# TensorE turns the identity matrix in front of its waits, and the norms turn early tiles whole

## The reference

```python
# first block
hn = rms_norm(h, mix_norm_pre);  proj = hn @ w_in          # 8 projections, 3272 columns
ret_out = retention(rope(rq), rope(rk), rv, rg)            # 8 heads, chunks of 128
att_out = dsa_attention(rope(aq), rope(ak), av, iq, ik, iw)  # top-k 128 keys per query, then softmax
h = h + rms_norm(concat(ret_out, att_out) @ w_out, mix_norm_post)
up = causal_dwconv(rms_norm(h, ffn_norm_pre) @ w_up)       # 2 x 2816 columns
h = h + rms_norm((silu(g) * u) @ w_down, ffn_norm_post)
# second block: every norm is followed by (1 + scale) and shift from c; every result gets a gate
x = x + gate * hgrn2_mixer(modulate(x));   x = x + gate * swiglu(modulate(x))
shared = nsa_shared_kv(modulate_kv(x))                     # compressed, selected and window keys
x = x + gate * nsa_mixer(modulate(x), shared);  x = x + gate * swiglu(modulate(x))
```

## Time and profile before

| | |
|---|---|
| median of 3 runs | 2125.06 us |
| profiled execution | 2125.37 us |
| its span | 2123.5 us, 30783 instructions |
| busy: PE, PE weight load, DVE, ACT, GpSimd | 2041.9, 1672.3, 1251.0, 798.1, 81.2 us |
| mean granted PE clock | 0.985 of 2.4 GHz |

### The profile page before, as it was taken

How to read it: one execution, slowest core, us unless ns; L and a number is a source line. 1 busy time by engine, 2 the same in 40 slices (tenths; PEclk the granted TensorE clock), 3 DMA queues, 4 the chain that set the end, 5 groups by cost and what they waited for, 6 DMA issues and landing times.

```text
span 2123.5 us, 30783 instructions
## 1 busy us (share of the span) xinstructions
PE 2041.9 (96%) x12072; PEld 1672.3 (79%) x12072; DVE 1251.0 (59%) x2209; ACT 798.1 (38%) x1455; POOL 81.2 (4%) x79
## 2 busy tenths in 40 slices
PE   7999899999999999999999999999899999999998
PEld 6688678888887877787888888779767678888887
DVE  4577757777745449755545545676777756322334
ACT  3323643333424552244222232433457743222222
POOL 1012000000000002000000000001001100000000
PEclk9999899999999999999999999999899999999999
DMA  6221024655442231202664644322300025233221
GB/s 209 96 83 41 18 92 160 199 191 166 159 148 90 90 100 62 81 21 90 199 197 159 203 153 166 122 84 79 122 1 2 2 79 166 92 100 99 99 90 50
DMA packets 146699, 231.48 MB, mean 109 GB/s; under 512 B 7325, under 2 KB 83709, under 8 KB 146557
## 3 DMA queue, kind: packets, MB, share of 16 engines
q1 hardware_dynamic: 144300, 224.05, 32.0%
q0 software_dynamic: 864, 3.15, 0.4%
q10 hardware_dynamic: 1392, 2.33, 0.3%
HBM read 227.41 MB, written 2.10 MB: 108 GB/s over the span
## 4 chain that ended last, share of the span: by engine, by line
PE 83%; DVE 9%; ACT 3%; issue 3%; POOL 0%; DMA 0%; ACTq 0%; DVEq 0%; POOLq 0%
PE ps L2304 11%; PE ps L2306 11%; PE ps L2305 11%; PE ps L2546 4%; PE ps L2331 4%; PE ps L2333 4%; PE ps L2332 4%; PE ps L2262 4%; PE ps L2264 4%; PE ps L2263 4%; PE ps L2544 3%; PE ps L2618 3%; PE ps L2387 2%; PE ps L2352 2%; PE ps L2364 2%
## 5 line engine op out<-in xcount | busy, mean ns | idle before, releaser
L1588 DVE TENSOR_TENSOR w_lo<-ring,w_hi 128x1024 fp32r<-128x1024 f32 (+4 forms) x362 | 376.9, 1043 | 701.8 <-ACT w_hi L990 701.2
L990 ACT ACTIVATE w_hi<-ring 128x1024 fp32r<-128x1024 f32 (+4 forms) x362 | 329.5, 912 | 970.5 <-PE ps L2306 471.9
L2304 PE MATMUL ps<-x_hi,w_hi 128*128 128x512 f32 x1056 | 416.5, 394 | 0.0
L2306 PE MATMUL ps<-x_hi,w_lo 128*128 128x512 f32 x1056 | 411.3, 389 | 0.0
L2305 PE MATMUL ps<-x_lo,w_hi 128*128 128x512 f32 x1056 | 411.2, 389 | 0.0
L2305 PEld LDWEIGHTS ps<-x_lo,w_hi 128*128 128x128 f32 x1056 | 198.6, 188 | 42.4 <-issue 1.9
L2304 PEld LDWEIGHTS ps<-x_hi,w_hi 128*128 128x128 f32 x1056 | 198.6, 188 | 42.3 <-issue 1.9
L2306 PEld LDWEIGHTS ps<-x_hi,w_lo 128*128 128x128 f32 x1056 | 198.3, 188 | 42.0
L2331 PE MATMUL ps<-w_hi,x_hi 128*128 128x512 f32 x480 | 187.5, 391 | 3.7 <-DVE x_hi L1664 3.7
L2333 PE MATMUL ps<-w_hi,x_hi 128*128 128x512 f32 x480 | 186.8, 389 | 0.0
L2332 PE MATMUL ps<-w_lo,x_hi 128*128 128x512 f32 x480 | 186.8, 389 | 0.0
(11 more groups left out here) (344 smaller groups left out, 2980.3 us busy)
## 6 DMA issues: line engine op xcount, KB each, us to landing
ring<-in_ada_w SPq DMA_DIRECT2D x48, 1024.0 KB, 5.0
ring<-in_ffn_w_in SPq DMA_DIRECT2D x88, 512.0 KB, 4.6
ring<-in_w_up SPq DMA_DIRECT2D x44, 512.0 KB, 4.6
ring<-in_ffn_w_out SPq DMA_DIRECT2D x20, 1024.0 KB, 4.7
ring<-in_hgrn_w_in SPq DMA_DIRECT2D x16, 1024.0 KB, 5.2
ring<-in_w_in SPq DMA_DIRECT2D x12, 1024.0 KB, 5.0
ring<-in_w_down SPq DMA_DIRECT2D x10, 1024.0 KB, 4.9
ring<-in_kv_ada_w SPq DMA_DIRECT2D x8, 1024.0 KB, 5.0
```

Of the source, the lines that this page charges most:

```text
L990: a.activation(to[:, n % depth, 0:src.shape[-1]], src, ACT.Copy).then_inc(s["hi_done"], 1)
L1588: v.tensor_tensor(to[:, n % depth, 0:width], src, hi[:, n % depth, 0:width].bitcast(F32), ALU.subtract).then_inc(s["lo_done"], 1)
L2304: mm(bs[j], wh[:, k, c], x_hi[:, 2 * q + k], start=first, stop=False)
L2306: ins = mm(bs[j], wl[:, k, c], x_hi[:, 2 * q + k], start=False, stop=last)
```

## The change

- `keep_busy(b, n, t)` turns the identity n times into a bank that PE holds anyway and that the next real result overwrites. It is put: in `norm`, ahead of the wait for a tile, by a table `BUSY`; ahead of the first piece of P1 (14), of the HGRN and NSA projections (12 each) and of each FFN (12); in the sparse attention ahead of each wait for an exponential (3) and of each pair of value products (3); in `q_turn` ahead of both turns (5 each); in the compressed groups ahead of the turn (6) and of the value product (4). Where a bank was opened behind a wait, it is opened ahead of it.
- `norm` turns channels 4 to 7 of tiles 0 and 1 once tile 1 is there, and all channels of tiles 2 and 3 as they come.
- The first FFN piece of unit 0 waits for one channel block, and goes through all four columns with it before the second block.
- Norm 0: `vec` moves to bank 7 and is turned behind tile 1; DVE copies it behind its second tile; ACT makes the second early `w_hi` behind channel block 1. The banks of P1's first unit are 0 to 3 in order.
- SP waits for x tile 1 before it issues the first weights. GpSimd issues its two rows after the rotation adds of P1.
- Norm 4: DVE no longer waits for the last turned block before it splits the first, and `XN[4]` lies in another part of the arena.

```diff
+            def keep_busy(b, n, t=0):
+                for _ in range(n):
+                    tr(b[:, t * P:(t + 1) * P], ident, ident)
...
+            BUSY = {0: (15, 0, 0, 0), 1: (0, 36, 0, 0), 2: (0, 36, 0, 0), 3: (0, 13, 7, 0), 4: (0, 0, 0, 13), 5: (0, 13, 7, 0)}
             def norm(i):
                 banks = [open_bank(("xT", i, kt)) for kt in range(4)]
-                for t in range(NT):
-                    pe.wait_ge(s["xn_ready"], NT * i + t + 1)
-                    for kt in range(4):
+                def tiles(t, kts):
+                    for kt in kts:
                         ins = tr(banks[kt][:, t * P:(t + 1) * P], XN[i][:, t, kt * P:(kt + 1) * P], ident)
                         if t == NT - 1:
                             ins.then_inc(full(("xT", i, kt)), 1)
-                for kt in range(4, KT):
-                    turn(lambda t: XN[i][:, t, kt * P:(kt + 1) * P], ("xT", i, kt))
+                for t in range(2):
+                    keep_busy(banks[0], BUSY[i][t], t)
+                    pe.wait_ge(s["xn_ready"], NT * i + t + 1)
+                    tiles(t, range(4))
+                if i == 0:
+                    vec_turn()
+                banks += [open_bank(("xT", i, kt)) for kt in range(4, KT)]
+                for t in range(2):
+                    tiles(t, range(4, KT))
+                for t in range(2, NT):
+                    keep_busy(banks[0], BUSY[i][t], t)
+                    pe.wait_ge(s["xn_ready"], NT * i + t + 1)
+                    tiles(t, range(KT))
...                                                        # ffn
+                        if (u, q) == (0, 0):
+                            keep_busy(open_bank(keys[0]), 12)
                         pe.wait_ge(s["lo_done"], n + 1)
-                        if u == 0:
+                        if u == 0 and q:
                             pe.wait_ge(s["x_split"], (KT + FT) * i + 2 * q + 2)
...
+                        if (u, q) == (0, 0):
+                            steps = [(j, k) for k in range(2) for j in range(4)]
+                        for j, k in steps:
+                            if (u, q) == (0, 0) and j == 0:
+                                pe.wait_ge(s["x_split"], (KT + FT) * i + k + 1)
...                                                        # attention
+                            if name == "dsa":
+                                keep_busy(b[:, at:], 3)
+                            pe.wait_ge(s["p_ready"], base + i + 1)
...
+                        if name == "dsa":
+                            keep_busy(b, 3, slot)
                         for q in range(2):
                             evacuated(pe, t_key(name, i + q, pair[q]["n"]))
...                                                        # P1, HGRN, NSA projections
+                    keep_busy(open_bank((name, 0)), 14)
+            keep_busy(open_bank((*H_UNITS[0], 0)), 12)
+            keep_busy(open_bank((*N_UNITS[0], 0)), 12)
...                                                        # q_turn, compressed groups
+                    b = open_bank(("nT", i, n))
+                    keep_busy(b, 5)
...
+                    b = open_bank(("cT", i - 1))
+                    keep_busy(b, 6)
...
+                    b = open_bank(("cO", i - 2))
+                    keep_busy(b, 4)
...                                                        # SP, ACT, DVE
+                if n == 0:
+                    sp.wait_ge(s["x_in1"], 16)
...
-                    early_highs(0, slice(0, 2))
+                    early_highs(0, slice(0, 1))
...
-                filled(dve, ("xT", i, KT - 1))
```

More of the change, by code:

```diff
@@ L270, in build @@
         INDEX_UNIT = P1_ORDER.index("rk")
-        plan_bank("vec")
+        plan_bank("vec", 7)
         def plan_norm(i):
@@ L397, in build @@
         plan_norm(0)
+        turn[0] = 1
         P1_PIECES = [(k, q) for k in range(len(P1_ORDER)) for q in range(4)]
@@ L406, in build @@
             for t in range(NT):
-                plan_bank((name, t), 4 * (k % 2) + ((t + 1) % NT if k == 0 else t))
+                plan_bank((name, t), 4 * (k % 2) + t)
             if k == 0:
@@ L957, in norm_out @@
                                      bias=0.0 if shift is None else shift[:, kt:kt + 1]).then_inc(free(("xT", i, kt)), 1)
+                        if kt == 1:
+                            early_highs(i, slice(1, 2) if i == 0 else slice(0, 0))
                     return
@@ L1372, in norm @@
                         x_normed(0, t)
+                        if t == 1:
+                            p = filled(dve, "vec")
+                            v.tensor_copy(vec[:, 0:CONV], p[:, 0:CONV]).then_inc(free("vec"), 1)
                 if i in MIXER_NORM:
@@ L2214, in _, with vec_turn @@
             tr = nc.tensor.transpose
+            def keep_busy(b, n, t=0):
+                for _ in range(n):
+                    tr(b[:, t * P:(t + 1) * P], ident, ident)
             pe.wait_ge(s["ident_in"], 16)
-            pe.wait_ge(s["vec_rows_in"], 16 * len(VEC_ROWS))
-            b = open_bank("vec")
-            tr(b[:, 0:64], vec_rows, ident[0:64, 0:64]).then_inc(full("vec"), 1)
+            def vec_turn():
+                pe.wait_ge(s["vec_rows_in"], 16 * len(VEC_ROWS))
+                b = open_bank("vec")
+                tr(b[:, 0:64], vec_rows, ident[0:64, 0:64]).then_inc(full("vec"), 1)
             def other_rows():
@@ L2293, in ffn @@
                         n = split_at[("up", i, u, q)]
+                        if (u, q) == (0, 0):
+                            keep_busy(open_bank(keys[0]), 12)
                         pe.wait_ge(s["lo_done"], n + 1)
-                        if u == 0:
+                        if u == 0 and q:
                             pe.wait_ge(s["x_split"], (KT + FT) * i + 2 * q + 2)
                         wh, wl = [w[:, n % 2].rearrange("p (k n) -> p k n", k=2) for w in (w_hi, w_lo)]
-                        for j in range(4):
-                            if q == 0:
+                        steps = [(j, k) for j in range(4) for k in range(2)]
+                        if (u, q) == (0, 0):
[3 more added lines that the diff above has]
+                                pe.wait_ge(s["x_split"], (KT + FT) * i + k + 1)
+                            if (q, k) == (0, 0):
                                 bs[j] = open_bank(keys[j])
                             c = slice(j * P, (j + 1) * P)
[L2302 to L2307, removed]
+                            first, last = (q, k) == (0, 0), (q, k) == (3, 1)
+                            mm(bs[j], wh[:, k, c], x_hi[:, 2 * q + k], start=first, stop=False)
+                            mm(bs[j], wh[:, k, c], x_lo[:, 2 * q + k], start=False, stop=False)
+                            ins = mm(bs[j], wl[:, k, c], x_hi[:, 2 * q + k], start=False, stop=last)
+                            if last and j < 3:
                                 ins.then_inc(full(keys[j]), 1)
```

17 lines of the change are left out of this document (6 added, 11 removed).

## The result

The changed kernel takes 2130.36 us (median of 16 runs, 2128.56 to 2134.08), the kernel before 2125.47 us (16 runs): a ratio of 1.0022, 95% interval 1.0014 to 1.0029. It is 4.9 us slower, where 0.0 was forecast. The range held it. The loss is clear of the noise, though smaller than the 0.3% that the prediction took as telling nothing. The profiled executions are 6.0 us apart in span, 2129.5 against 2123.5.

What follows compares the result with a forecast made beforehand. PE, busy for 96% of the span, was taken as the bound. Start −4.7, norm hand-overs −6.0, sparse attention +5.3, NSA preparation with compressed groups +5.4 sum to 0.0: 2125.0 us forecast, range 2118 to 2133.

Steps and rivals of the forecast that it cites:

- Sparse attention: Sparse attention, 144 identity turns: forecast +5.3 us, bounds −1.2 (all hidden) and +15.8 (none).
- the turns of the first four groups lie in waits of PE: Sparse attention: identity turns of the early groups cost nothing; only 3 later groups of 18 are on the path, 5.9 us.
- DVE's 95%: Sparse attention, 206.50 to 229.00: DVE busy for 21.33 of 22.50 us, with the top-k search and the maxima.
- the 0.4 us that was taken off for the low clock: Sparse attention, early stretch: low clock costs at most 1.2 us, of which 0.4 was taken as gain.
- Norm 4: Hand-over at norm 4: first block 1.6 us later, against DVE no longer waiting for the last block; −0.5 us.
- ACT's evictions then set the pace: Norm 4: ACT's two evictions per block set the pace, giving −0.5 us.
- Hand-overs 1, 2, 3, 5: Hand-overs at norms 1, 2, 3 and 5: first matmuls start sooner; −0.95, −0.85, −1.45 and −2.3 us.
- Start: Kernel start: first matmul at 16.6 instead of 19.56 (−3.0), wait ahead of fourth `iq` result goes by bank order (−1.7); −4.7 us.
- Preparation and groups: NSA preparation 3.3 us less 1.4 for the clock, compressed groups 3.5 with turns 3.2 us apart; +5.4 us.
- Clock: Whole kernel: turns bring the clock up; granted clock 1.00 throughout but at norm 4 and the HGRN part.
- Rival C: Five norms: identity turns don't hold the clock, 3.5 us each, 17.5 us slower in all, 2142; chance 0.07.
- rival D: PE bounds attention two groups earlier (36 turns, 4.0 us); preparation's clock falls anyway (3.3 us more); 2132; chance 0.13.

Runs made afterwards that it cites:

- e12: The changed kernel with six identity turns in place of three at each place in the sparse attention, 288 in all; 2142.58 us, ratio 1.0082.
- e7: The changed kernel without norm 4's 13 identity turns ahead of the last tile, its new order of turns kept; 2127.97 us, ratio 1.0008.
- e4: The changed kernel with no identity turn anywhere, all its other edits kept; 2120.68 us, ratio 0.9971.
- e11: The kernel of e9 with the start's transfers as before: first weights not waiting for x tile 1, broadcast rows at the head of GpSimd's queue; 2115.39 us.
- e10: The kernel of e9 with the bank order of the first P1 unit as in the kernel before (fourth result in bank 0); 2111.53 us.
- e5: The changed kernel without identity turns in sparse attention, query turns and compressed groups, and norm 4 in old order without identity turns; 2113.33 us, ratio 0.9942.
- e6: The changed kernel with identity turns in the sparse attention only for units 16 to 31, the later half; 2127.77 us, ratio 1.0007.
- e8: The kernel of e5 plus the ten identity turns of each of the query turns 4 to 7; 2111.23 us, ratio 0.9930.
- e2: The changed kernel with norm 4 alone back in its old order of turns, without its 13 and twelve identity turns; 2126.83 us, ratio 1.0001.
- e9: The kernel of e8 plus four identity turns ahead of each probability turn of the compressed groups; 2110.73 us, ratio 0.9928.
- e1: The changed kernel without the 144 identity turns of the sparse attention; 2122.18 us, ratio 0.9980.

## Why the prediction was wrong, point by point

**The bound**: right. PE holds the chain, and at full clock an added turn costs 0.11 us wherever PE has no wait (e12: 5.91 us for 54).

**Sparse attention**: the step that failed was "the turns of the first four groups lie in waits of PE". It rested on DVE's 95% and priced 18 turns a group at full clock. DVE is the busier engine there, but it takes its turn with PE: score product, maximum, turn, copy. In the first group, at low clock, 18 turns take 3.8 us (0.64 for three), and the two waits of PE that they could lie in were 0.97 and 0.50 us before (the score products' own waits come earlier). In the third, PE was busy for all of its 5.60 us before. In all five groups PE's busy time rose by 8.9 us (22.8 to 31.7), of which waits took 4.6. And the 0.4 us that was taken off for the low clock did not come. Measured +10.1: 5.8 late, 4.3 early.

**Norm 4**: "the first block comes 1.6 us later; against that DVE no longer waits ... −0.5". Both halves of the mechanism were right; the delay was mis-sized. The block came 4.2 us later, 2.1 by the identity turns and 2.1 by the order (e7), in which the turns of tiles 0 and 1 wait for banks that DVE's gain sums still hold (1.22 us) and then stand ahead of the last tile at half clock. That ACT's evictions then set the pace was wrong: from the first matmul to the key turns the stage took 114.9 us before and changed, and PE waited for ACT for 0.4 us of it. Measured +2.2, and −2.1 with the old order.

**Hand-overs 1, 2, 3, 5**: −0.95, −0.85, −1.45, −2.3 forecast, −0.89, −0.78, −1.20, −2.11 measured. Right, but at 3 and 5 the identity turns have hardly a part in it, 0.1 us each (e4).

**Start**: right in sign, 1.3 us short. First matmul at 16.07 (15.5 to 17.7 named). Transfers −3.0 by e11, as forecast. The 1.3 us beyond the forecast are 0.5 ahead of the first matmul and 0.8 behind it, where a second wait for ACT of 0.8 us went beside that of 1.73. For the larger wait the bank order was the wrong reason (e10). Unforeseen was also the clock: without the 29 identity turns the attention comes 2.7 us later (e4); but in the execution of e5 the same turns didn't bring the clock up in time.

**Preparation and groups**: +5.4 forecast, +4.3 measured: +1.9 up to the first group turn, as forecast; the groups came to 3.07 us apart, not 3.2, and to +2.4 in place of +3.5.

**Clock**: that turns hold the clock up was right at norms 1 and 2, where it fell without them (e4). At norm 1, 36 identity turns took 4.09 us at a granted clock of 1.00. It did not hold everywhere: in the sparse attention, which the prediction had at 1.00, the clock fell for 6.8 us at 202.7. The Trainium skill (TensorE: Matmul & The Clock Gate, Part 4: PE-mode transpose) has transpose mode as not engaging the full clock; these runs disagree, for identity operands as for data. Rival C is out. Of rival D the first half has the size (36 more turns on the path, 4.0 us; measured 4.3) but not the place: 2.7 us of it lie in the first group, not in the two groups ahead of the late ones. Its second half doesn't hold: in the preparation the clock stayed full.

**Open**: HGRN's small products took 0.8 us more in the changed kernel, e6, e7, e8, e10 and e11, and not in the others, with the same instructions (3.66 in place of 3.62 us a round). Their cause wasn't found. About 1.6 us is also paid for a fall of 3.4 us, which comes near 943, near 1700, or at both:

```profile
939.60:946.00 6.40, 4.71 (x21) 3.95 (x22) 4.73 (x7) 2.98 (x12) 0.00 (x0) 1.00 0.01 4
1701.70:1705.10 3.40, 3.40 (x16) 3.11 (x15) 3.40 (x6) 2.80 (x5) 0.00 (x0) 0.52 0.00 0
```

(the kernel of e2, which has the second alone; e5 had both, e8 and e11 neither). What moves it wasn't settled.

## What to carry to other kernels

Filler on an engine is free only where that engine waits, and only for as long as it waits: add up its own waits group by group ahead of each filler, at the clock of that stretch. Another engine's busy share doesn't answer this, since two engines that hand work to each other can both be the bound. Take each place of such a change by itself, too: here three parts cost 20 us, each taken alone. Without them the kernel is 12 us faster than before (e5), and 15 us with a few turns put back where PE waits (e9).

## What was not expected of the hardware

- It matters where the half clock falls more than how long it lasts. 17.1 us of it early in the attention left the stretch at 53.15 us (e1), 13.7 us at 53.14 (e9) and 53.27 (before). In e5, e10 and e11 it was shorter or as long (17.0, 13.6 and 13.6 us), but its last 3.4 us came at the end of the fifth window or across it, where PE had no wait, and the stretch took 54.91, 54.78 and 54.50.
- At norms 3 and 5 the clock stayed at 1.00 in e4, without identity turns; data turns that had moved into the waits stood there in their place.
- The same instructions at the start don't always meet the same clock: 24 turns of norm 0 took 2.84 us in the changed kernel and 4.56 in e5, with nothing changed ahead of them.
